# Attention on one core: five PSUM banks for scores in rotation and two slots for turned probabilities, in place of four banks in a fixed pattern and three slots

## What is computed

```python
sc = einsum('bhqd,bhkd->bhqk', qi, k) * scale       # 128 queries, dq = 96, up to 2048 keys
sc = where(key_chunk[None, :] <= qc[:, None], sc, -inf)   # chunks of 64: block causal
p  = softmax(sc, axis=-1)
o  = einsum('bhqk,bhkd->bhqd', p, v)                # v: 64 wide
```

## Time and profile before

| | us |
|---|---|
| time, median of 3 runs | 2318.33 (2317.79 to 2319.71) |
| the profiled execution, whole | 2320.45 |
| its span | 2318.7 |
| TensorE busy in the span | 2193.0 (95%) |
| mean granted clock of TensorE | 0.978 |

### The profile page before, as it was taken

How to read it: one execution, slowest core, us unless ns; L and a number is a source line. 1 busy time by engine, 2 the same in 40 slices (tenths; PEclk the granted TensorE clock), 3 DMA queues, 4 the chain that set the end, 5 groups by cost and what they waited for, 6 DMA issues and landing times. The chain is left out here.

```text
span 2318.7 us, 32825 instructions
## 1 busy us (share of the span) xinstructions
PE 2193.0 (95%) x11569; PEld 1815.4 (78%) x11569; DVE 1051.5 (45%) x1875; ACT 902.9 (39%) x1676; POOL 342.1 (15%) x326
## 2 busy tenths in 40 slices
PE   7999999999989999999978989999999998999998
PEld 6888887778868888888856767778888777778886
DVE  6111000100014555544436656777777776664652
ACT  7212111100113444443433325566666665443441
POOL 1221214032201111111111330000000022000000
PEclk9999999999989999999989998999999999999999
DMA  5222122231312323333256764333213336574751
GB/s 188 81 70 77 59 80 73 86 110 59 113 47 80 95 90 99 95 100 95 73 194 229 266 194 102 71 71 73 44 39 69 73 98 203 175 224 131 206 155 64
DMA packets 215331, 257.99 MB, mean 111 GB/s; under 512 B 37712, under 2 KB 136464, under 8 KB 212752
## 3 DMA queue, kind: packets, MB, share of 16 engines
q1 hardware_dynamic: 186000, 203.59, 30.9%
q10 hardware_dynamic: 23552, 42.50, 4.9%
q0 software_dynamic: 5696, 10.79, 1.7%
HBM read 159.28 MB, written 97.54 MB: 111 GB/s over the span
## 5 line engine op out<-in xcount | busy, mean ns | idle before, releaser
L74 PE MATMUL bankD<-hT_hi,shared_w_hi 128*128 128x512 f32 x512 | 212.5, 415 | 7.2 <-POOLq L870 7.2
L76 PE MATMUL bankD<-hT_hi,shared_w_lo 128*128 128x512 f32 x512 | 201.9, 394 | 0.0
L75 PE MATMUL bankD<-hT_lo,shared_w_hi 128*128 128x512 f32 x512 | 201.1, 393 | 0.0
L74 PE MATMUL bankA<-hT_hi,shared_w_hi 128*128 128x512 f32 x512 | 200.9, 392 | 0.0
L76 PE MATMUL bankA<-hT_hi,shared_w_lo 128*128 128x512 f32 x512 | 199.6, 390 | 0.0
L75 PE MATMUL bankA<-hT_lo,shared_w_hi 128*128 128x512 f32 x512 | 199.5, 390 | 0.0
L1845 DVE TENSOR_REDUCE small_chunk_min<-scores 128x1 f32<-128x512 f32 (+2 forms) x320 | 180.9, 605 | 36.1 <-PE scores L76 22.3
L1865 ACT ACTIVATE probs<-scores,small_least 128x1024 f32<-128x1024 f32 (+2 forms) x192 | 167.3, 871 | 12.5 <-DVE small_least L1852 11.4
L74 PE MATMUL bankA<-wt_hi,hT_hi 128*128 128x512 f32 x384 | 150.7, 392 | 4.2 <-DVE shared_v_raw L498 2.5
L1999 DVE TENSOR_TENSOR pT<-turn_rest,pT 128x512 fp32r<-128x512 f32 (+2 forms) x208 | 126.2, 624 | 53.2 <-ACT pT L1965 53.2
L75 PE MATMUL bankA<-wt_lo,hT_hi 128*128 128x512 f32 x384 | 150.1, 391 | 0.0
(11 more groups left out here) (267 smaller groups left out, 4659.9 us busy)
## 6 DMA issues: line engine op xcount, KB each, us to landing
shared_w_raw<-in_w_in_dram SPq DMA_DIRECT2D x32, 512.0 KB, 4.4
projT<-stage ACTq DMA_DIRECT2D x64, 256.0 KB, 2.4
projT<-d_stage ACTq DMA_DIRECT2D x64, 256.0 KB, 2.4
e_l_in<-projT SPq DMA_DIRECT2D x64, 256.0 KB, 4.9
gateTok<-stage ACTq DMA_DIRECT2D x32, 256.0 KB, 2.0
shared_w_lo<-hgTok SPq DMA_DIRECT2D x16, 512.0 KB, 3.4
knT<-b_out SPq DMA_DIRECT2D x32, 256.0 KB, 3.6
vTok<-b_out SPq DMA_DIRECT2D x32, 256.0 KB, 4.5
```

The source lines that it names most:

```text
L74: pe.matmul(out, a_hi, b_hi, start=first, stop=False)
L75: pe.matmul(out, a_hi, b_lo, start=False, stop=False)
L76: return pe.matmul(out, a_lo, b_hi, start=False, stop=last)
```

## The change

`SCORE_RING` is 5: chunk number n of a head (0 to 39, in order) uses bank (n + 2) mod 5, and 40 chunks a head make the rotation go on from head to head. The fifth bank is taken from the turn slots, of which two remain. The cut between the two pieces of a row goes where the rotation comes back to bank 0, or after two chunks. `pieces_before` looks up the last use over all rows. A slot use `at` needs use `at - 2` read. Since `TURN_RING` is 2, the third tile of a step is transposed behind the values of the step before. The last latent projections lose one bank.

```diff
-            return e % RING if e < E_LAST else (0, 1, 6, 7)[(e - E_LAST) % 4]
+            return e % RING if e < E_LAST else (0, 1, 7)[(e - E_LAST) % 3]
...
-TURN_RING = 3
+TURN_RING = 2
+SCORE_RING = 5
...
     def s_bank(i, c):
-
-        b, r = i // TPB, i % TPB
-        return (c + (r if b == 0 else 2 * (r % 2) if b == 1 else 3 * r if b == 2 else 0)) % 4
+        return (CHUNK_AT[i, c] + 2) % SCORE_RING
...
-        cut = min(1 if s_bank(i, 0) == 3 else 2, b + 1)
+        cut = next((c for c in range(1, b + 1) if s_bank(i, c) == 0), min(2, b + 1))
...
-        need = 0
-        for (t, piece), at in PIECE_AT.items():
-            if t < i:
-                used = {s_bank(t, x) for x in range(*chunks_of(t, piece))}
-                if s_bank(i, c) in used:
-                    need = max(need, at + 1)
-        return need or PIECE_AT[TT - 1, s_bank(i, c) // 2] + 1 - PIECES
+        def last_use(rows):
+            return max((at + 1 for (t, piece), at in PIECE_AT.items()
+                        if t in rows and s_bank(i, c) in [s_bank(t, x) for x in range(*chunks_of(t, piece))]), default=0)
+
+        return last_use(range(i)) or last_use(range(i, TT)) - PIECES
...
-        scores = ctx.enter_context(nc.psum_tensor("scores", [P, 4, BLK], F32))
-        turn_rest = ctx.enter_context(nc.psum_tensor("turn_rest", [P, 2, BLK], F32))
-        turn = [turn_first[:], turn_rest[:, 0], turn_rest[:, 1]]
+        scores = ctx.enter_context(nc.psum_tensor("scores", [P, SCORE_RING, BLK], F32))
+        turn_rest = ctx.enter_context(nc.psum_tensor("turn_rest", [P, BLK], F32))
+        turn = [turn_first[:], turn_rest[:]]
...
-                if at < 3:
-                    pe.wait_ge(turn_read, h * TURNS + 1)
-                else:
-                    pe.wait_ge(turn_read, h * TURNS + (at - 1))
+                if h * TURNS + at > 0:
+                    pe.wait_ge(turn_read, h * TURNS + at)
...
-                        pe.wait_ge(turn_read, h * TURNS + (at - 1))
+                        pe.wait_ge(turn_read, h * TURNS + at)
```

## The result

| us | kernel before | changed kernel |
|---|---|---|
| median, 17 runs each | 2318.37 | 2327.58 |
| ratio | | 1.0024, 95% interval [1.0013, 1.0035] |
| a second comparison (`after_again`) | | 1.0014 [1.0000, 1.0028] |
| profiled execution, span | 2318.7 | 2320.8 |
| mean granted clock, profile | 0.978 | 0.982 |

What follows compares the result with a forecast made beforehand. TensorE, busy 95% of the span, was taken to bound the kernel. Six middle heads 6.9, first head 0, last 3.8 and clock 1.4 summed to +12.1 us: 2330.4 us as median, forecast range 2323 to 2339, overall 2319.5 to 2340.

Steps and rivals of the forecast that it cites:

- The price of a slot, 2.15 us, and where it is covered: Transposes: a slot is free 2.15 us after its tile's start; some six value matmuls ahead cover a step's third tile.
- those of u38, u41 and u42: Rows 7 and 8: u38 waits 0.5, u41 and u42 together 0.5, mostly replacing old waits; net +0.1 us.
- One head, +1.15: Each middle head: steps sum to +1.15 us, bounds +0.4 and +1.8, against some 2.8 us of score-bank waits gone.
- -0.2 + 0.55: First head behind row 12: what is left of the list of steps, -0.2 and +0.55 us.
- row 15's late 1408-wide piece: Row 15: its last two chunks wait for piece 14.1, now 1408 wide; no wait taken, at most 0.5 us.
- The last head, +3.8: Last head: no scores behind row 15 cover its slots; 0.6 + 3.2 = +3.8 us, four steps 2.15 apart, not 1.88.
- The 2.96 are swallowed; I take -0.5: First head: row 8's 2.96 us wait goes, but row 12's wait for its queries' DMA absorbs it; -0.5 us there.
- one of the signs of being wrong that the prediction named: Wrong if u6 doesn't wait, bank waits over 1 us remain at rows 11 to 14, or first head's gain passes row 12.
- The clock, +1.4: Head boundaries: new waits close together make TensorE's clock fall at one boundary more; +1.4 us, bounds 0 and +6.
- the rule cited there: Trainium skill on TensorE's clock: throttled is the default state and activity releases it; all seven boundaries might show a fall.
- Four of the seven boundaries: Profile of the kernel before: four of seven head boundaries show the clock's fall, costing 1.4 us in the head examined.
- The rival of no change: Middle heads: new and old waits cancel, only the tail's 3 us remain; 2319 to 2323 us, chance 0.12.

Runs made afterwards that it cites:

- `after_again`: The changed kernel, unaltered, run once more against the kernel before: 2323.96 us, ratio 1.0014 [1.0000, 1.0028].
- `four_banks_two_slots`: The kernel before with its four score banks, but two turn slots and the new order of a step's third tile: 2335.51 us, ratio 1.0066.
- `first_wait_back`: The changed kernel, with row 8 of the first head again waiting before its last chunk for row 7's exponentials: 2327.25 us, ratio 1.0028.
- `third_tile_early`: The changed kernel, with the third tile of a step transposed ahead of the values, as in the old order: 2370.33 us, ratio 1.0223.
- `before_again`: The kernel before, unaltered, run once more: 2322.18 us, ratio 1.0009 [0.9997, 1.0021].
- `old_first_tile_ahead`: The kernel before, four banks and three slots, with tile u0 alone turned ahead of row 9's scores: 2325.96 us, ratio 1.0025.

## Why the prediction came out as it did

- **The price of a slot, 2.15 us, and where it is covered: right.** Every wait named is there, the 29.3 us of bank waits went down to the 2.35 before row 9 of the first head, and slot waits rose. The total was under-counted: 35 to 45 us were forecast, 53.6 at transposes and 4.7 at folds (2.8 and 1.9, the latter in a line not shown) are there. The count left out waits that only take the place of old ones, as those of u38, u41 and u42.
- **One head, +1.15: right (1.09).** So was the reason: `four_banks_two_slots` shows 1.8 lost to slots and 0.75 won from banks. The first head behind row 12 came out at +0.36 (1460.79 - 1408.76 = 52.03, against 51.67) in the first two profiles, both of which have a fall there, where -0.2 + 0.55 was forecast. That row 15's late 1408-wide piece holds nothing up was right as well.
- **The last head, +3.8: mechanism right, term too high** (3.3). Its steps run 2.07 us apart (1925.91 to 1927.98), not 2.15.
- **The first head: wrong step, "The 2.96 are swallowed; I take -0.5".** It treated the DMA as fixed ("moved by 0 to 1 us at most") and took the wait for it as a sink. Row 12's wait did not grow to 5; it is 3.17. In the kernel before, the loads of its keys and queries were issued late partly because row 8 was late: 0.9 us, shown by `first_wait_back`. Row 12 comes 2.0 us earlier in the mean of eight against eight profiles, and 3.1 in the two pairs of the kernels themselves; what goes beyond 0.9 is scatter of the transfer and the clock. That the first head's gain reaches row 12 is one of the signs of being wrong that the prediction named. It also overlooked that row 9 now waits for 7.0, 2.35 us, as the table of the waits says.
- **The clock, +1.4: wrong sign.** This was the largest miss: -5.9 us by the lengths of heads 2 to 8, 7 away from the term. I argued that more waits near the boundary mean more falls. But the old order already shows falls behind 10 of 14 heads, with its own waits, and the new one behind 3 of 14; and `third_tile_early`, with the most waiting of all, shows none in its middle heads. By the rule cited there all seven boundaries might have shown one; the trace doesn't agree. A single profile with falls at "Four of the seven boundaries" was no basis for a term, as its repetition had six. Why the changed order has fewer falls stays open.
- The sum from measured terms: 6 x 1.09 + 3.3 - 5.9 for the clock in heads 2 to 8, and -0.7 for the first head as a whole (-3.1 to row 12, +2.4 behind it, where both changed profiles have a fall and one of the two before): +3.2 us, against 4.4 measured, within what these terms are known to.
- The rival of no change (2319 to 2323) came near for the wrong reason. Counted from 2318.33, the 4.4 us give 2322.7, at its upper end; the median of the changed kernel, 2327.58, lies among the forecast's 2323 to 2339. The heads did get longer, and what cancelled was mainly a term that neither named.

## What to carry to other kernels

Before a buffer moves from one ring to another, measure the round trip of both and list for each use what work stands between it and the use that it must follow; the uses without cover are the price, and waits won elsewhere count only where they don't stand just behind a wait that stays. A wait for a DMA swallows a gain ahead of it only if nothing in the DMA's own chain stood behind the work that moved, so follow the chain through every engine's queue. A term for the clock needs several profiles of the kernel before, and its sign should be left open.

## What the runs showed of the hardware

I had not expected that TensorE's clock could answer to work that lies far from the waits. In the fall shown above the granted clock is 0.83 over 10 us, part of it at 1.2 instead of 2.4 GHz. Middle heads with a mean granted clock of 0.97 or 0.98 are 0.9 to 1.5 us longer than those without a fall, those with 0.95 are 1.6 to 2.2 us longer, those with 0.93 3.4 to 4.7 us. Ten repeated transposes in the middle of a head went with two heads with a fall in place of four and six, and with a mean clock of 0.9792 against 0.9772. In the old order a head with one fall takes 67.9 to 68.2 us, and such heads come in a row (six in `before_again`, with the last head); in the kernels with third tiles among the scores the heads with falls are 68.3 to 68.4 and 71.6 to 71.7 long, and come in a row too; in the changed kernel they are 69.2 to 69.3, and a middle head behind one has none.

The Trainium skill, "TensorE: Matmul & The Clock Gate", section "What's actually happening", says that the monitor of activity is free-running and does not reset when a kernel starts, so that the moment of a change of the clock depends on when the work lands. My guess from it is that certain lengths of a loop repeat their falls. That heads with falls gather at a few lengths fits it. But heads of 67.6 us go with a mean clock of 0.9766 in `old_first_tile_ahead` and heads of 67.8 us with 0.9804 and 0.9813 in the changed kernel, and no run here was made to test it.
